# Moving weights in the compression's first linear, finishing steps inside linears, and six leading chunks in the output linear

## What is computed

```
proj = h @ w_in            # fox q,k,v; forget gate; nsa q; six nsa k/v; gates
kc, vc = compress(kc), compress(vc)
    # 31 windows of 32 tokens, stride 16, of t + pos_emb, per group g of 2:
    # gelu(flat(2048) @ w1 (2048x256) + b1) @ w2 (256x64) + b2
y_a = fox attention ; y_b = nsa attention (compressed, selected, window)
mixed = sigmoid(gate_a) * (y_a @ w_o_fox) + sigmoid(gate_b) * (y_b @ w_o_nsa)
x = x + mixed @ w_out
x = x + square(relu(rmsnorm(x) @ w_up)) @ w_down
```

## Time and profile before

| | us |
|---|---|
| median of 3 runs | 2231.97 (2231.52 to 2234.8) |
| profiled execution, its own time | 2231.35 |
| its span | 2229.6 |
| PE busy / POOL busy / DVE busy / ACT busy in the span | 2198.7 / 1500.5 / 1162.8 / 607.4 |
| mean granted TensorE clock | 0.999 |

### The profile page before, as it was taken

One profiled execution on the slowest core, in us unless ns is written; L12 is line 12 of the kernel. 1 busy time (PEld: TensorE's weight loads), 2 busy tenths in 40 slices (PEclk: granted clock), 3 DMA queues, 4 the chain that ended last, 5 costly groups with the idle time before them and its releaser, 6 DMA issues.

```text
span 2229.6 us, 29899 instructions
## 1 busy us (share of the span) xinstructions
PE 2198.7 (99%) x11018; PEld 1751.1 (79%) x11019; DVE 1162.8 (52%) x1934; ACT 607.4 (27%) x1435; POOL 1500.5 (67%) x679
## 2 busy tenths in 40 slices
PE   9999999999999999999999999999999999999998
PEld 6876788888887867778788888878677787888886
DVE  8769667773353285557640243552665477411422
ACT  5248222221021165531220121111455412200210
POOL 7650687778875614448887888756334488888884
PEclk9999999999999999999999999999999999999999
DMA  5320233333323301112333333233111123333332
GB/s 193 111 76 1 76 95 95 97 102 97 111 95 114 114 29 58 51 54 95 95 103 96 95 96 103 86 113 114 58 39 58 58 84 93 99 101 95 95 98 73
DMA packets 54921, 195.79 MB, mean 88 GB/s; under 512 B 7312, under 2 KB 7312, under 8 KB 54544
## 3 DMA queue, kind: packets, MB, share of 16 engines
q1 hardware_dynamic: 52496, 187.85, 26.5%
q10 hardware_dynamic: 2304, 6.22, 0.8%
HBM read 191.82 MB, written 2.10 MB: 87 GB/s over the span
## 4 chain that ended last, share of the span: by engine, by line
PE 90%; DVE 6%; issue 2%; ACT 1%; DMA 0%; POOL 0%; SPq 0%; DVEq 0%
PE bank L491 25%; PE bank L493 25%; PE bank L492 25%; PE bank L606 3%; PE bank L616 3%; PE bank L653 1%; DVE t L1292 1%; PE bank L507 1%; PE bank L577 1%; PE bank L635 1%; DVE prow L1405 1%; PE bank L656 1%; DVE bank L1394 1%; PE bank L568 1%; ACT prow L1016 1%
## 5 line engine op out<-in xcount | busy, mean ns | idle before, releaser
L436 POOL TENSOR_TENSOR w_hi<-w_raw,zero 128x1024 fp32r<-128x1024 f32 x336 | 657.4, 1957 | 677.0 <-PE bank L493 663.4
L439 POOL TENSOR_TENSOR w_lo<-w_raw,w_hi 128x1024 fp32r<-128x1024 f32 x336 | 844.6, 2514 | 26.5
L491 PE MATMUL bank<-hn_hi,w_hi 128*128 128x512 f32 x1632 | 648.9, 398 | 6.4 <-POOL w_lo L439 3.2
L493 PE MATMUL bank<-hn_hi,w_lo 128*128 128x512 f32 x1632 | 636.2, 390 | 0.0
L492 PE MATMUL bank<-hn_lo,w_hi 128*128 128x512 f32 x1632 | 635.9, 390 | 0.0
L491 PEld LDWEIGHTS bank<-hn_hi,w_hi 128*128 128x128 f32 x1632 | 306.6, 188 | 76.5 <-issue 8.3
L492 PEld LDWEIGHTS bank<-hn_lo,w_hi 128*128 128x128 f32 x1632 | 306.8, 188 | 64.2 <-issue 3.4
L493 PEld LDWEIGHTS bank<-hn_hi,w_lo 128*128 128x128 f32 x1632 | 306.5, 188 | 64.5
L491 PE MATMUL bank<-hid_hi,w_hi 128*128 128x512 f32 x688 | 267.9, 389 | 0.0
L493 PE MATMUL bank<-hid_hi,w_lo 128*128 128x512 f32 x688 | 267.8, 389 | 0.0
L492 PE MATMUL bank<-hid_lo,w_hi 128*128 128x512 f32 x688 | 267.8, 389 | 0.0
(11 more groups left out here) (294 smaller groups left out, 2666.3 us busy)
## 6 DMA issues: line engine op xcount, KB each, us to landing
w_raw<-wstream SPq DMA_DIRECT2D x352, 512.0 KB, 3.5
x<-xT SPq DMA_DIRECT2D x4, 512.0 KB, 7.7
out<-yout ACTq DMA_DIRECT2D x8, 256.0 KB, 2.2
mem_x<-memT SPq DMA_DIRECT2D x1, 1024.0 KB, 12.7
lnc<-lncount ACTq DMA_DIRECT2D x1, 1024.0 KB, 5.6
cs<-trig ACTq DMA_DIRECT2D x2, 512.0 KB, 4.3
par<-params ACTq DMA_DIRECT2D x1, 696.0 KB, 5.6
bc<-bconst ACTq DMA_DIRECT2D x1, 664.0 KB, 6.8
```

The costliest lines, as they stand in the source:

```text
L436: nc.gpsimd.tensor_tensor(w_hi[:, slot, :], w_raw[:, slot, :], zeros, ALU.add).then_inc(w_rounded, 1)
L439: nc.gpsimd.tensor_tensor(w_lo[:, slot, :], w_raw[:, slot, :], w_hi[:, slot, :].bitcast(f32), ALU.subtract).then_inc(w_split, 1)
L491: nc.tensor.matmul(ps[bank][:, 0:cols_], wh, a_h, start=c == 0, stop=False)
L493: mm = nc.tensor.matmul(ps[bank][:, 0:cols_], wl, a_h, start=False, stop=c == chunks - 1)
```

## The change

It does three things. First, in the compression's first linear cmp_g becomes the stationary operand, padded from 62 to 64 columns, and the weights move, 256 columns (all hidden units) per chunk. A raw half is now four chunks of 128 rows. Even chunks accumulate in rows 0 to 63 of bank 7, odd ones in rows 64 to 127, the key in columns 0 to 255, the value in the others. The host reorders the w1 blocks for that. When both tiles of a key or value are done, ACT copies the bank to w1sum, and PE multiplies it by a constant, fold (`fold_w1`, in the middle of the linear at i = 15 and 25), which adds the two row halves and turns the result; then ACT does the two gelus. Second, the finishing step of the tile ahead of a w1 tile moves from behind that raw half to the middle of the next linear (`finish`). Third, the output linear's first two tiles are no longer a strict pair: six chunks of the first, two of the second, two of the first, six of the second.

```diff
-        cmp_g = at("cmp_g", [2, 1024], f32, R + 70 * KIB)
+        cmp_g = at("cmp_g", [2, 16, 64], f32, R + 70 * KIB)
+        w1sum = at("w1sum", [256], f32, R + 62 * KIB)
...
+        fold = fc[:, 5 * P + S + 32:5 * P + S + 32 + 2 * NCMP]
...
-                ph["in"].append(tile("w1", n, c, 4))
+                ph["in"].append(tile("w1", n, c, 4, 7))
...
@@ -496,18 +498,23 @@
 
             def linear_w1(t, half):
 
-                kind, n, block_, _, bank, _, _ = tiles[t]
-                if half == 0:
-                    pe.wait_ge(*took(last_on_bank[bank]))
-                    last_on_bank[bank] = t
-                for c in range(8 * half, 8 * half + 8):
-                    b_, j = block_ + c // 8 * 3, c % 8
-                    if j == 0:
-                        pe.wait_ge(w_split, b_ + 1)
-                    mm = nc.tensor.matmul(ps[bank][:, 0:2 * NCMP], w_raw[:, b_ % RING, j * P:(j + 1) * P],
-                                          cmp_g[:, n // 2, c * 2 * NCMP:(c + 1) * 2 * NCMP], start=c == 0, stop=c == 15)
-                    if j == 7:
-                        mm.then_inc(blocks_done, 1)
+                _, n, block_, _, bank, _, _ = tiles[t]
+                kv, b_, q = n // 2, block_ + 3 * half, 2 * (n % 2) + half
+                pe.wait_ge(w_split, b_ + 1)
+                for c in range(4 * q, 4 * q + 4):
+                    rows, j = slice(64 * (c % 2), 64 * (c % 2) + 64), c % 4
+                    mm = nc.tensor.matmul(ps[bank][rows, kv * 256:(kv + 1) * 256], cmp_g[:, kv, c, :],
+                                          w_raw[:, b_ % RING, j * 256:(j + 1) * 256], start=c < 2, stop=c >= 14)
+                mm.then_inc(blocks_done, 1)
+
+            def fold_w1(l, kv):
+
+                pe.wait_ge(w1_kept, 2 * l + kv + 1)
+                for f in range(2):
+                    a_ = P + (2 * kv + f) * 2 * NCMP
+                    mm = nc.tensor.matmul(ps[4][:, a_:a_ + 2 * NCMP], w1sum[:, f * P:(f + 1) * P], fold,
+                                          start=True, stop=True)
+                mm.then_inc(w1_folded, 1)
...
@@ -853,17 +860,34 @@
                 ph = LIN[l]
                 jobs = ph["in"]
                 on_bank = {tiles[t][4]: t for t in jobs}
-                spare = (norm_rt, 4 + 2 * l)
+                spare = (w1_kept, 2 * l + 2)
                 first_free = [spare if b == 7 else took(on_bank[b]) for b in ((2, 7, 0, 1) if l == 0 else (0, 1, 2, 7))]
+                def finish(m):
+
+                    nonlocal roped_n, v_done
+                    t = jobs[m]
+                    kind = tiles[t][0]
+                    if kind in ("qr", "kr"):
+                        pe.wait_ge(rope_in, 6 * l + idx_of_rope(t) + 1)
+                        rotate(roped_n, tmp[:, roped_n % 2, :])
+                        roped_n += 1
+                    if kind == "v":
+                        pe.wait_ge(*took(t))
+                        pe.wait_ge(v_kept, v_done)
+                        turn_tile(sq[:, v_done % 2, :], 6, TT).then_inc(v_turned, 1)
+                        v_done += 1
+
                 for i in range(len(jobs) + 2):
                     if i == 0:
                         pe.wait_ge(mask_loaded, 16)
                     if i < len(jobs) and tiles[jobs[i]][0] == "w1":
+                        if tiles[jobs[i]][1] == 0:
+                            pe.wait_ge(norm_rt, 4 + 2 * l)
...
+                    elif i < len(jobs) - 1 and i > 2 and tiles[jobs[i - 1]][0] == "w1":
+                        linear(jobs[i], hn_hi, hn_lo, S, DC, part=(0, 4))
+                        finish(i - 2)
+                        linear(jobs[i], hn_hi, hn_lo, S, DC, part=(4, DC))
+                    elif i in (15, 25):
+                        linear(jobs[i], hn_hi, hn_lo, S, DC, part=(0, 4))
+                        if i == 15:
+                            pe.wait_ge(fg_parts, l + 1)
+                        fold_w1(l, i // 25)
+                        linear(jobs[i], hn_hi, hn_lo, S, DC, part=(4, DC))
                     elif 1 < i < len(jobs):
                         linear(jobs[i], hn_hi, hn_lo, S, DC)
                         if tiles[jobs[i - 2]][0] == "w1":
                             linear_w1(jobs[i - 2], 1)
-                    if 0 <= i - 1 < len(jobs):
-                        t = jobs[i - 1]
-                        kind = tiles[t][0]
-                        if kind in ("qr", "kr"):
-                            pe.wait_ge(rope_in, 6 * l + idx_of_rope(t) + 1)
-                            rotate(roped_n, tmp[:, roped_n % 2, :])
-                            roped_n += 1
-                        if kind == "v":
-                            pe.wait_ge(*took(t))
-                            pe.wait_ge(v_kept, v_done)
-                            turn_tile(sq[:, v_done % 2, :], 6, TT).then_inc(v_turned, 1)
-                            v_done += 1
+                    if 0 <= i - 1 < len(jobs) and not (i < len(jobs) and tiles[jobs[i]][0] == "w1"):
+                        finish(i - 1)
...
-                        pe.wait_ge(fg_parts, l + 1)
...
-                linear_pair(ph["out"][0], ph["out"][1], mx_hi, mx_lo, (mix_split, DC * l))
+                first, second = ph["out"][0:2]
+                linear(first, mx_hi, mx_lo, S, DC, (mix_split, DC * l), part=(0, 6))
+                linear(second, mx_hi, mx_lo, S, DC, part=(0, 2))
+                linear(first, mx_hi, mx_lo, S, DC, (mix_split, DC * l), part=(6, DC))
+                linear(second, mx_hi, mx_lo, S, DC, part=(2, DC))
...
-                    if i >= 2 and tiles[jobs[i - 2]][0] == "w1":
+                    if i >= 2 and tiles[jobs[i - 2]][0] == "w1" and tiles[jobs[i - 2]][1] % 2:
                         t = jobs[i - 2]
-                        idx = tiles[t][1]
+                        kv = tiles[t][1] // 2
                         act.wait_ge(blocks_done, filled(t))
-                        A(hidc[:, idx // 2, idx % 2, :], ps[tiles[t][4]][:, 0:2 * NCMP], ACT.Gelu_apprx_tanh,
-                          bias=pcol(f"b1_{'kv'[idx // 2]}{l}", idx % 2)).then_inc(w1_took, 1)
+                        A(w1sum[:, :], ps[7][:, kv * 256:(kv + 1) * 256], ACT.Copy).then_inc(w1_kept, 1)
+                        act.wait_ge(w1_folded, 2 * l + kv + 1)
+                        for f in range(2):
+                            a_ = P + (2 * kv + f) * 2 * NCMP
+                            A(hidc[:, kv, f, :], ps[4][:, a_:a_ + 2 * NCMP], ACT.Gelu_apprx_tanh,
+                              bias=pcol(f"b1_{'kv'[kv]}{l}", f)).then_inc(w1_took, 1)
...
+                V.memset(cmp_g[:, :, :, 2 * NCMP:], 0.0)
...
-                            d = cmp_g[:, kv, 0:16 * 62].rearrange("p (j g n) -> p j g n", j=16, g=2)[:, :, g, :]
+                            d = cmp_g[:, kv, :, g * NCMP:(g + 1) * NCMP]
...
-        w1 = [_blocks(a) for a in i["cmp_w1_2"][l]]
+        w1 = [a.reshape(4, 4, P, 256).transpose(0, 2, 1, 3).reshape(4, P, 1024) for a in i["cmp_w1_2"][l]]
...
+    both = ((p[:, None] % 64 == n[None, :]) & (n[None, :] < 2 * NCMP)).astype(f)
```

More of the change, by code:

```diff
@@ L172, in build @@
         Q += (NPAR * 4 + 31) // 32 * 32
-        fc = at("fc", [5 * P + S + 32], f32, Q)
-        Q += (5 * P + S + 32) * 4
+        fc = at("fc", [5 * P + S + 96], f32, Q)
+        Q += (5 * P + S + 96) * 4
         bc = at("bc", [5 * P + 4 * 248 + 8 * P], bf16, Q)
@@ L217, in build @@
             sem(n) for n in ("trig_angle", "trig_filled", "trig_packed", "trig_ready"))
-        norm_gx, w1_took = sem("norm_gx"), sem("w1_took")
+        norm_gx, w1_took, w1_kept, w1_folded = sem("norm_gx"), sem("w1_took"), sem("w1_kept"), sem("w1_folded")
         scored, row_min, row_exp, row_sum, p_scaled, p_turned, p_kept, pv_done = (
@@ L555, in norm_spread, with linear_pair @@
                 mm.then_inc(norm_row, 1)
-            def linear_pair(ta, tb, hi, lo, ready, n=None):
+            def linear_pair(ta, tb, ready, n=None):
                 for c in range(DC):
-                    linear(ta, hi, lo, S, DC, ready, part=(c, c + 1))
-                    linear(tb, hi, lo, S, DC, part=(c, c + 1))
+                    linear(ta, hn_hi, hn_lo, S, DC, ready, part=(c, c + 1))
+                    linear(tb, hn_hi, hn_lo, S, DC, part=(c, c + 1))
                     if n is not None and c == 3:
@@ L843, in _ @@
                 linear(t, mix_hi, mix_lo, S, DC)
-            linear_pair(UP1[0], UP1[1], hn_hi, hn_lo, (norm_lo, 2 * DC), 2)
+            linear_pair(UP1[0], UP1[1], (norm_lo, 2 * DC), 2)
             for t in UP1[2:]:
@@ L865, in _ @@
                     elif i == 0:
-                        linear_pair(jobs[0], jobs[1], hn_hi, hn_lo, (norm_lo, DC * (3 + 2 * l)), 3 + 2 * l)
+                        linear_pair(jobs[0], jobs[1], (norm_lo, DC * (3 + 2 * l)), 3 + 2 * l)
                     elif i == len(jobs) - 1:
@@ L936, in _ @@
                     if half == 0:
-                        linear_pair(up[0], up[1], hn_hi, hn_lo, (norm_lo, DC * (4 + 2 * l)), 4 + 2 * l)
```

(5 more changed lines are left out.)

## The result

| | before | after |
|---|---|---|
| median, us (range) | 2231.78 (2231.52 to 2234.8) | 2217.51 (2217.0 to 2218.76) |
| profiled execution / its span, us | 2231.35 / 2229.6 | 2217.0 / 2215.2 |

A forecast was written before the change was run, and what follows sets the result against it. PE, start to start of its instructions, was taken to bound the kernel. Terms -10.1 + 2.2 + 0.1 - 1.5 + 0.4 - 0.8 - 3.0 = -12.7 us gave 2219.3 us (chance 0.58), range 2215.5 to 2224.5.

The forecast's parts named there:

- Raw halves: Compression's first linear: 16 halves fall from 1.73 to 1.10 us each, 10.1 us off.
- the v turns' new borders: Two v turns per layer each get one more border between f32 and the linear: 4 x 0.1 = 0.4 us added.
- the stall: Rotation of qr 3 behind tile 1's raw half waits for DVE, once per layer: 2 x 0.74 = 1.5 us off.
- Fold: Adding the two row halves on PE amid a linear, without waiting: 4 x 0.55 = 2.2 us added.
- Finishing steps: Moving them from behind the raw half into the next linear: 1.5 us off for the rotation's wait, 0.4 added for borders.
- Bank wait: Layer 0's output linear: second tile no longer waits for the bank DVE's last mix step reads, 0.76 us off, once.
- norm_rows: Up pair: POOL splits earlier, DVE's chain from output tile 6 takes 11.7 us instead of 13.2; 2 x 1.5 = 3.0 off.
- Rival B: At norm_rows PE alone decides, not DVE's chain: 2217.6 us; chance 0.09.
- Rival A: DVE's chain keeps its length, norm_rows stays 13.2 us behind tile 6 and PE waits there: 2222.3 us; chance 0.20.
- C: The fold waits because ACT gets to copy or gelu late, up to 0.9 us at four folds: 2222.9 us; chance 0.07.
- D: The raw halves' matmul pairs don't overlap, so a half takes 1.88 us: 2231.8 us; chance 0.04.
- E: Each change of row half drains the array, 0.396 us per recorded matmul: 2252.4 us, slower; chance 0.02.

The follow-up runs named there:

- one chunk pair later: Changed kernel with the norm's row matmuls (norm_rows) one chunk pair later inside each shared first pair of tiles: 2215.32 us, ratio to before 0.9921.
- the kernel with one row half: Changed kernel with all 16 chunks of a compression matrix summed in rows 0 to 63, no alternating: 2232.88 us, ratio to before 1.0004.

## Why the prediction was right

**Raw halves.** 1.10 us each, with the border ahead, was forecast and is what the rows show. Two readings in the prediction are loose. Its 0.43 us for a 512-column f32 matmul is the price of a record: the rotation at 699.63 is one matmul, recorded twice, and holds PE for 0.86. And the last four records of the earlier trace rows take 0.07 over half of 0.92, not 0.10. The first changes no sum, since a half is counted as eight records; the second is small. The sum over all f32 steps set into layer 0's input linears (from the last linear matmul ahead of each to the third behind it, less the pitches) went down by 4.4 us: 4.65 for the halves with the v turns' new borders (forecast 4.85), 0.70 for the stall (0.74), and 0.92 up for two folds (1.1).

**Fold.** Forecast 0.55, measured 0.46, with no wait.

**Finishing steps.** The price of 1.1 us was right against the kernel before, and that is how the sum was made; as the change holds all its parts, the total comes out whichever part is credited. But the text gives the halves their 10.1 us without saying that they need this part: 3.3 us of them go into new or longer waits without it, as the kernel without the moved steps shows, and with the old stalls that comes to the 4.8 us above. The prediction looked at who hides work, and not at who waits behind a half that gets shorter.

**Bank wait.** 0.84 us off against 0.76, mx in time.

**norm_rows.** Place and mechanism were right, the size was off: the term "2 x 1.5 = 3.0 off" measured 3.86. The chain from the end of tile 6 (1061.20, a block before up's start) to norm_rows takes 11.3 us, not 11.7, before 13.2. The forecast had hn_lo end at 8.6, POOL's last pass run from 8.7 to 11.0 behind it, and the sum end at 11.6. Measured, hn_lo ended at 8.4, the pass ran from 7.9 (1069.12) to 10.65, and the sum ended at 11.2. So the pass took longer than foreseen, 2.73 us for 2.3, and the size was off because it began 0.8 us earlier: it started before hn_lo's end and not behind it. Rival B's figure (2217.6) is nearly the measured one, but its mechanism isn't shown: DVE still decided, or one chunk pair later would have gained nothing. Rival A is refuted by every kernel with the new order. On the Trainium skill's rule of the port pair (SBUF — State Buffer) the rows agree. The sum t takes 0.68 us where it begins ahead of a pass (1066.62), and the pass that begins during it takes 2.16 us instead of 1.89. Begun behind the start of a pass (1069.52) the same sum takes 2.88 and ends 0.55 us behind that pass; at half speed it would have taken some 1.4 (an estimate from the 0.68).

**C, D and E.** C is refuted by the fold's row, which has no idle time ahead, D and E by the halves' rows; the kernel with one row half shows what D would have cost.

**What the sum left out.** Two small pieces, 1.0 us together, favoured the change and are not its terms. At 79 us the changed kernel is 0.5 us ahead; in the twelve traces of the experiments the same point scatters between -0.4 and +0.4 us of before, whatever the kernel. And in layer 1's attention 0.5 us went where PE waits for ACT. Before:
```profile
1583.05 0.34 PE L592 MATMUL bank<-c,bc 96*128 96x384 bf16 x1 [0.21 <-ACT prow L1016]
1583.72 0.34 PE L592 MATMUL bank<-c,bc 96*128 96x384 bf16 x1 [0.33 <-ACT prow L1016]
```
and after:
```profile
1570.69 0.34 PE L599 MATMUL bank<-c,bc 96*128 96x384 bf16 x1
1571.29 0.34 PE L599 MATMUL bank<-c,bc 96*128 96x384 bf16 x1 [0.26 <-ACT prow L1043]
```
This piece belongs to the moving weights and the fold: every kernel here that has them shows the second pair of rows, also the one with one row half, and the kernels with the output order or the finishing steps alone show the first pair. The prediction put nothing there. What ACT was late with wasn't tried.

## What to carry to other kernels

When a step gets shorter, look at what stands behind it and by whom its operand is made: if that was just in time, the saving becomes a wait (here a move that was worth 1 us by itself was worth 5 behind shorter halves). Two f32 products of 64 output rows run side by side if they alternate between row halves, and of the moving weights only this paid here. A wait that the profile shows as 0.2 us between pipelined matmuls may be 0.4: subtract starts and compare with the pitch.

## What the runs showed of the hardware

**A short fall of the clock moves 1.7 us in some executions.** In the trace of the kernel with the output order alone, PE's scores in layer 1's attention take 2.42 us; the changed kernel's, same form, take 1.35 in layer 0.
```profile
1586.42 2.42 PE L606 MATMUL bank<-ka,qa 64*128 64x128 f32 x8
```
```profile
790.65 1.35 PE L613 MATMUL bank<-ka,qa 64*128 64x128 f32 x8
```
Two stretches of the kernel with the output order alone (length, PE, PEld, DVE, ACT, POOL busy, granted clock, DMA share, GB/s):
```profile
1580.00:1586.00 6.00, 4.26 (x25) 2.17 (x25) 5.64 (x22) 5.08 (x18) 1.12 (x1) 1.00 0.28 89
1586.00:1590.00 4.00, 3.90 (x15) 2.17 (x16) 3.08 (x12) 1.70 (x8) 0.00 (x0) 0.57 0.02 4
```
In these 4 us a share of 0.57 was granted, so most of them at the lower of the two levels, 1.2 GHz (share 0.5), and (1 - 0.57) x 4 = 1.7 us of PE's work are lost. It follows a stretch in which PE was busy 4.26 of 6 us. The kernel before is as little busy at the same place (4.31 of 6 us from 1583 on) and its clock stays at 2.4 GHz:
```profile
1583.00:1589.00 6.00, 4.31 (x26) 2.41 (x28) 5.61 (x22) 4.96 (x17) 0.44 (x1) 1.00 0.24 87
1589.00:1593.00 4.00, 4.00 (x40) 2.76 (x38) 3.66 (x16) 2.92 (x10) 0.00 (x0) 1.00 0.02 4
```
Of the 14 profiled executions, seven show such a fall at the start of layer 0's or layer 1's attention, and those of before and after don't. One more, that of the kernel with moving weights, fold and finishing steps, shows one at 11 us, and its PE is no later at 79 us for it. So the totals of two single traces can differ by 1.7 us for a reason that has nothing to do with the kernels; phases compared one by one leave it out. The Trainium skill (TensorE: Matmul & The Clock Gate, Part 1: The HAM clock gate) says that the gate that follows PE's activity knows these two levels only; the 0.57 doesn't speak against it, since it is a mean over a stretch with the change in it.

**Matmuls over 64 rows cost more than over 128, amid a linear.** The four records of a fold cost PE 0.80 us with 64 rows and 0.46 with 128. They stand among 128-row matmuls in both kernels, so whether the matmuls themselves are slower or the change of shape costs is open.
